# Delta-rule inverse: query decays by chunk, value rows behind x, state scalings over five levels

## The reference, cut to what matters

```python
a_mat = where(strict, einsum('bhnid,bhnjd->bhnij', kb, kc) * dmat, 0.0)
rhs = concatenate([vc * bc[..., None], kb * exp(gc)[..., None]], axis=-1)
sol = triangular_solve(a_mat + eye(l), rhs, left_side=True, lower=True, unit_diagonal=True)
q_dec = qc * exp(gc)[..., None]
...
v_new = u_i - einsum('bhck,bhkv->bhcv', w_i, s)
o = einsum('bhck,bhkv->bhcv', q_i, s) + einsum('bhij,bhjv->bhiv', qk_i, v_new)
s = s * gl[..., None, None] + einsum('bhck,bhcv->bhkv', k_i, v_new)
```

## Time and profile before

| | |
|---|---|
| median of 3 runs | 1632.32 us (1630.23 to 1634.59) |
| the profiled execution | 1632.61 us |
| its span in the trace | 1630.9 us |
| busy share of PE, PEld, DVE, ACT, POOL | 97%, 91%, 63%, 53%, 15% |
| granted TensorE clock, mean | 0.992 of full speed |
| inversion, GDN layer one | 137.7 to 177.2 us of the span |
| inversion, GDN layer two | 1338.9 to 1378.5 us of the span |

### The profile page before, as it was taken

One profiled execution on the slowest core, in us unless ns is written; L12 is line 12 of the kernel. 1 busy time (PEld: TensorE's weight loads), 2 busy tenths in 40 slices (PEclk: granted clock), 3 DMA queues, 4 the chain that ended last, 5 costly groups with the idle time before them and its releaser, 6 DMA issues.

```text
span 1630.9 us, 37346 instructions
## 1 busy us (share of the span) xinstructions
PE 1574.7 (97%) x16067; PEld 1483.1 (91%) x16067; DVE 1019.6 (63%) x1684; ACT 856.8 (53%) x1647; POOL 250.8 (15%) x319
## 2 busy tenths in 40 slices
PE   7999999999999999999999999999999999999997
PEld 6998799999997999997788887999989997899997
DVE  6965677745757877544372656776448937777653
ACT  5756656633635666431531546665347647566533
POOL 6005450000110200002002330200010016500000
PEclk9999999999999999999999999999999999999999
DMA  8941455565743655653633202655558623455550
GB/s 220 283 157 41 118 155 180 182 203 182 245 144 130 196 181 181 206 176 72 185 94 106 53 4 64 181 181 197 184 148 250 177 89 96 129 175 181 183 180 27
DMA packets 245528, 250.09 MB, mean 153 GB/s; under 512 B 16270, under 2 KB 239284, under 8 KB 245300
## 3 DMA queue, kind: packets, MB, share of 16 engines
q1 hardware_dynamic: 237040, 224.74, 44.8%
q0 software_dynamic: 8016, 22.86, 4.7%
q10 hardware_dynamic: 308, 0.10, 0.0%
HBM read 229.75 MB, written 18.32 MB: 152 GB/s over the span
## 4 chain that ended last, share of the span: by engine, by line
PE 90%; ACT 4%; DVE 4%; issue 1%; DMA 0%; SPq 0%; DVEq 0%
PE ps L771 86%; PE ps L775 4%; DVE acts L2551 1%; ACT vk L1906 1%; ACT acts L1906 1%; ACT tri L1906 1%; ACT st L1906 0%; DVE hn L2551 0%; DVE acts L2543 0%; DVE tri L2543 0%; ACT hn L1906 0%; DVE st L2551 0%; DMA acts<-in_x_sample_dram 0%; ACT w_gdn L1906 0%; DVE mixer_lo L2543 0%
## 5 line engine op out<-in xcount | busy, mean ns | idle before, releaser
L2543 DVE TENSOR_TENSOR w_mlp<-ring,w_mlp 128x1024 fp32r<-128x1024 f32 x256 | 311.6, 1224 | 121.7 <-ACT w_mlp L1906 115.7
L1906 ACT ACTIVATE w_mlp<-ring 128x1024 fp32r<-128x1024 f32 x256 | 269.3, 1054 | 211.5 <-PE ps L771 211.5
L771 PE MATMUL ps<-hn_split,w_mlp 128*128 128x264 f32 x3072 | 373.3, 284 | 0.0
L771 PE MATMUL ps<-h_split,w_mlp 128*128 128x264 f32 x3072 | 372.6, 283 | 0.0
L771 PEld LDWEIGHTS ps<-hn_split,w_mlp 128*128 128x128 f32 x3072 | 372.0, 188 | 0.3
L771 PEld LDWEIGHTS ps<-h_split,w_mlp 128*128 128x128 f32 x3072 | 371.6, 188 | 0.0
L771 PE MATMUL ps<-gdn_hi,w_gdn 128*128 128x264 f32 x1024 | 194.8, 289 | 7.3 <-DVE mixer_lo L2543 7.2
L1906 ACT ACTIVATE tri<-ps 128x264 f32<-128x264 f32 (+4 forms) x226 | 103.5, 466 | 181.8 <-PE ps L771 156.2
L771 PEld LDWEIGHTS ps<-gdn_hi,w_gdn 128*128 128x128 f32 x1024 | 162.4, 190 | 11.0 <-issue 8.9
L771 PE MATMUL ps<-mixer_lo,w_gdn 128*128 128x264 f32 x512 | 146.4, 286 | 0.0
L1906 ACT ACTIVATE acts<-ps 128x264 f32<-128x264 f32 (+6 forms) x116 | 49.8, 431 | 176.8 <-PE ps L771 175.5
(11 more groups left out here) (405 smaller groups left out, 2372.1 us busy)
## 6 DMA issues: line engine op xcount, KB each, us to landing
ring<-in_ffn_w_dram SPq DMA_DIRECT2D x128, 1024.0 KB, 5.4
ring<-in_gdn_w_in_dram SPq DMA_DIRECT2D x32, 1024.0 KB, 6.1
ring<-in_ml_w_in_dram SPq DMA_DIRECT2D x12, 1024.0 KB, 5.4
ring<-in_rw_w_rkv_dram SPq DMA_DIRECT2D x12, 1024.0 KB, 5.3
st<-in_state_gdn_S_dram POOLq DMA_DIRECT2D x2, 4096.0 KB, 23.5
ring<-in_gdn_w_out_dram SPq DMA_DIRECT2D x8, 1024.0 KB, 5.0
out_gdn_S_s_dram<-st SPq DMA_DIRECT2D x16, 512.0 KB, 4.5
st<-in_state_mlstm_C_dram POOLq DMA_DIRECT2D x1, 4096.0 KB, 19.9
```

What stands on the lines that cost most here:

```text
L771: return nc.tensor.matmul(out, lhsT, rhs, start=start, stop=stop)
L1906: return nc.scalar.activation(out, in_, f, bias=bias, scale=scale)
L2543: return nc.vector.tensor_tensor(out, in0, in1, op)
```

## The change

Three edits, all inside the inversion of the GDN layers. ACT's state scalings, 32 in all, are drawn from one list in the same order of heads, and spread thus: at level 1 two at (1, 0), none at (1, 1), four at (1, 3); at levels 2, 3 and 4 two at (l, 0), two at (l, 1), two at (l, 3); at level 5 four at (5, 0) and four at (5, 1). The value rows of chunks 1 to 3 move from (l, 1) to (l, 3), behind `new_half`; those of chunk 0 stay at (1, 1). POOL scales its heads 0, 1 and 2 after the masks of levels 1, 2 and 3, decays the queries of chunks 1 and 2 after those of level 4, and those of chunk 3 and its head 3 after those of level 5; a decay by chunk is one instruction of 128x512, and chunk 0 is no longer decayed. PE waits for each chunk's own.

```diff
-                    if c == 1:
-                        pe.wait_ge(qs_ok, count.seen(qs_ok, 4))
+                    pe.wait_ge(qs_ok, count.seen(qs_ok))
...
-                def scale_states(h, part):
-                    for s in range(4 * part, 4 * part + 4):
+                scalings = iter([(h, s) for h in range(4, GH) for s in range(NS)])
+
+                def scale_states(n):
+                    for h, s in islice(scalings, n):
                         last = act(st[:, s * GH + h, :], st[:, s * GH + h, :], ACT.Copy, scale=E6[:, 4, h * NS + s:h * NS + s + 1])
-                    if part:
-                        last.then_inc(sts_ac, count.up(sts_ac))
+                        if s == NS - 1:
+                            last.then_inc(sts_ac, count.up(sts_ac))
...
-                    fills[l, 0] = lambda l=l: scale_states(3 + l, 0)
-                    fills[l, 1] = lambda l=l: value_rows(l - 1)
-                    fills[l, 3] = lambda l=l: scale_states(3 + l, 1)
+                    fills[l, 0] = lambda: scale_states(2)
+                    fills[l, 1] = lambda: scale_states(2)
+                    fills[l, 3] = lambda l=l: (value_rows(l - 1), scale_states(2))
                 fills[1, 1] = lambda: (sample_squares(), value_rows(0))
-                fills[1, 3] = lambda: (sample_norm(), scale_states(4, 1))
+                fills[1, 3] = lambda: (sample_norm(), scale_states(4))
+                fills[5, 0] = fills[5, 1] = lambda: scale_states(4)
...
+                def decayed_states(h):
+                    gp_.tensor_tensor(sth[:, h], sth[:, h], bc(E6[:, 4, h * NS:(h + 1) * NS], P, 2), ALU.mult).then_inc(
+                        st_sc, count.up(st_sc))
+
+                def decayed_queries(c):
+                    queries = acts[:, 4 * (c // 2):4 * (c // 2) + 4, c % 2 * P:(c % 2 + 1) * P].rearrange("p h (g t) -> p g h t", g=2)
+                    part = QS[:, :, c * HD:(c + 1) * HD].rearrange("p (g h) t -> p g h t", g=2)
+                    gp_.tensor_tensor(part, part, queries, ALU.mult).then_inc(qs_ok, count.up(qs_ok))
...
-                    if 1 <= l < 5:
-                        if l == 1:
-                            po.wait_ge(smp_ev, count.seen(smp_ev))
-                        po.wait_ge(eq_ev, count.seen(eq_ev))
-                        for h in (2 * l - 2, 2 * l - 1):
-                            part = QS[:, h, :].rearrange("p (a b t) -> p a b t", a=2, b=2)
-                            last = gp_.tensor_tensor(part, part, rows_of(0, h), ALU.mult)
-                        last.then_inc(qs_ok, count.up(qs_ok))
-                        s_ = sth[:, l - 1]
-                        gp_.tensor_tensor(s_, s_, bc(E6[:, 4, (l - 1) * NS:l * NS], P, 2), ALU.mult).then_inc(
-                            st_sc, count.up(st_sc))
+                    if l == 1:
+                        po.wait_ge(smp_ev, count.seen(smp_ev))
+                    elif l == 4:
+                        po.wait_ge(eq_ev, count.seen(eq_ev, 4))
+                    if l in (1, 2, 3):
+                        decayed_states(l - 1)
+                    elif l == 4:
+                        decayed_queries(1)
+                        decayed_queries(2)
+                    elif l == 5:
+                        decayed_queries(3)
+                        decayed_states(3)
```

More of the change, by code:

```diff
@@ L3 @@
 from contextlib import ExitStack
+from itertools import islice
 import math
```

## The result

| | before | changed |
|---|---|---|
| median (beside one another) | 1632.11 us, 6 runs | 1643.61 us, 6 runs |
| lowest to highest | 1630.23 to 1634.59 us | 1638.87 to 1647.31 us |
| profiled execution, its span | 1632.61 us, 1630.9 us | 1641.70 us, 1640.0 us |
| mean granted TensorE clock of that profile | 0.992 | 0.986 |

The ratio is 1.0064, 95% interval 1.0049 to 1.0079: slower, +10.5 us by the ratio, where +1.3 us was forecast. The range ended at 1637.0 us.

A forecast was written before the change was run, and what follows sets the result against it. PE was taken to carry 90% of the chain of waits; per layer +0.83 (level 5) - 0.13 (level 2) - 0.03 (value rows) = +0.67 us, two layers +1.3 us, giving 1633.6 us on the median, range 1630.0 to 1637.0 us.

The forecast's parts named there:

- a shift at the inversion's end is a shift of the end: PE's work after the inversion: comes one piece behind the other, so the end moves by the inversion's shift.
- moves with PE by the same amount, not more: Work behind level 5, such as `solve_values(0)` and state stores: later only by PE's own delay, 0.83 us.
- Level 5: Inversion's level 5: eight added ACT scalings start `turned_half(1)` 0.83 us later, all on the path, per layer.
- The margins of levels 3 and 4: `turned_half(0)` at levels 3 and 4: 0.05 us to spare, so no cost; up to 0.1 us each if missed.
- Value rows: ACT's value rows ahead of `new_half(0)`: PE's product comes last, so moving them gains only 0.03 us per layer.
- Level 2: Inversion's level 2: fewer scalings free `turned_half(1)` before PE's eight transposes end, gaining 0.13 us per layer.
- Rival (a): Level 2: POOL's state scaling holds DVE off by 1.89 us at most, +0.2 us per layer, 1634.0 us; chance 0.10.
- the sign that I had named: Level 2, PE's eight transposes to the half product into bank 5: the distance 1.15 us becomes 1.02.
- POOL: POOL's decays by chunk, taken at 1.4 us each, stay hidden; level 5's masks in time, a gap after level 3.
- Sum of the waits: Both inversions: +0.83 at level 5, -0.13 at level 2, -0.03 for value rows, +0.67 us per layer, +1.3 us.
- (d): Inversion: ACT bounds every level and all level 5 scalings lie in the path, 3.5 us per layer, 1639.3 us; chance 0.05.
- same: Whole kernel: no change that can be told, within about 0.3% or 4.9 us; chance 0.92.

The follow-up runs named there:

- e7: Changed kernel with seven 128x128 identity products on PE ahead of level 5's third half product; 1635.11 us, ratio 1.0011.
- e9: Kernel before with 4 and 6 identity products in PE's two waits ahead of each output projection; 1629.84 us, ratio 0.9985.
- e10: Changed kernel with three 128x128 identity products on PE ahead of level 5's third half product; 1635.52 us, ratio 1.0016.
- e6: Kernel before with 8 and 12 identity products in PE's two waits ahead of each output projection; 1633.50 us, ratio 1.0002.
- e3: Changed kernel with PE repeating level 5's third half product twice more on the same data; 1639.37 us, ratio 1.0031.
- e11: Changed kernel measured again, unaltered; 1643.29 us, ratio 1.0058 to the kernel before.
- e4: Kernel before with head 7's eight state scalings moved from level 4 to level 5, six at (5, 0), two at (5, 1); 1639.12 us, ratio 1.0035.
- e8: Kernel before with head 7's eight scalings moved to level 5, three at (5, 0), five at (5, 1); 1633.45 us, ratio 1.0000.
- e1: Changed kernel with ScalarE's order of before, so POOL's edits alone; 1634.44 us, ratio 1.0010.
- e5: Changed kernel with ScalarE's scalings all within levels 1 to 4, none in level 5; 1633.44 us, ratio 1.0005.
- e12: e9 with e5's spread of ScalarE's scalings, value rows behind x and POOL's order of before; 1627.35 us, ratio 0.9972.

## Why the prediction was wrong

The step that failed stands in two places, in the first paragraph, "a shift at the inversion's end is a shift of the end", and at the end of the level 5 part, where what is behind "moves with PE by the same amount, not more". Matmuls behind the shift were taken at the durations of the kernel before, and they depend on what PE did just ahead. What the runs showed in its place: behind the lengthened wait the clock can fall to half for 10 to 14 us, which in the profiled run moved what follows inversion two by 6.1 us more than the wait. I had the granted clock in the page, 0.992, and did not ask where the missing part stood: much of it stood behind waits of PE (1.24 and 1.77 us before the projections, 2.77 us before 750 us, 3.11 us before 1222 us), and the change made one more. Why such a wait makes the clock fall in one run and not in the next stays open.

- **Level 5**: right in place and size (4.22 us forecast, 4.20 measured; the idle wait is there). The margins of levels 3 and 4 held (5.92 and 5.91 us from level to level, 5.90 and 5.91 before).
- **Value rows**: right, the 1.61 us distance is unchanged.
- **Level 2**: wrong in sign, +0.12 instead of -0.13 us. Rival (a)'s mechanism was real, and the forecast put it at nothing. It held DVE off by 1.07 us at the masked values, and I had sought its price at the subtractions; it came at bank 7, whose keys DVE makes before them. That the rival's size, 0.2 us, is near the 0.25 us between the two signs is luck. So is the sign that I had named: the distance did become 158.17 - 157.15 = 1.02 us, but because the transposes at its start were late. The rule of the Trainium skill (SBUF — State Buffer, Who interferes with whom) is borne out: DVE's 0.48 us instruction with two inputs in SBUF became 2.00.
- **POOL**: right in what it hides; two decays by chunk took 2.51 us, so 1.25 each where I took 1.4, the masks of level 5 in time, the gap after level 3 there.
- **Sum of the waits**: +1.3 forecast, +2.1 measured in the profile. Within the range.
- **What was missing**: a term for the fall, 6.1 us in this profile, and by the mean clock there was one or more in 12 of 14 runs of the changed kernel. None of the rivals had it; (d), the slow one, was priced by another mechanism, at 5%. The chance of "same", 0.92, rested on the belief that there was nothing else. Of the signs that were to show the forecast wrong (shrunken distances of 1.61 us, longer levels 3 and 4, a wait for a mask) none appeared: all looked at waits, none at the clock.

## What to carry to other kernels

A wait of under a microsecond on PE can cost several times its length. Here it stood in a stretch of small matmuls and short gaps; whether that is needed was not tried. Before pricing a delay there, look up where the granted clock is below full in the kernel at hand, and what PE did ahead of it. Such a cost is a chance per run, so one profile doesn't size it; the mean granted clock of each run, read beside its time, comes nearer, though it mixes this stretch with all others. Where PE must wait anyway, a few full matmuls into a free bank kept the clock here (e7, e9, e10), and they paid only where the wait held them (e9 against e6).

## What the runs showed of the hardware that was not expected

- A fall to the half clock followed on 0.62 us (e3, layer one) to 0.90 us (changed and e11, layer two) of idle PE behind the inversion's stretch of 64x64 products with gaps of 0.45 us; behind 0.86 us (changed, layer one) and 1.05 us (e4, layer two) it did not come in the profiled run. With 0.17 us (e8) no run showed it. It lasted 10 to 14 us under a PE that was busy without a gap.
- One and the same wait of 3.91 us at the start of the program is followed by 10 us at half clock in some profiles (e1, e7, e10) and by the full clock in others (before, e5).
- The order before is not wholly free of falls behind an inversion: e9, whose inversion is that of the kernel before, shows one short stretch behind inversion two:

```profile
1380.00:1384.00 4.00, 4.00 (x42) 0.59 1.00 282
```

- With 0.7 us of the wait filled with 128x128 products no run of 12 showed the long fall; with 0.24 us of 32-row products at least 4 of 12 did. Whether rows, duration or the idle remainder of 0.62 us decides was not tried.
- In some profiles (e1, e9, e12, layer one) PE sat idle for 0.42 or 0.43 us between the two halves of level 5's second product with no releaser that the profile shows; its cause stays open.
